# Expert layer of a hybrid decoder step: the last two experts' gate/up weights ahead of both their down weights

## The chip, the cores and the metric

The kernel runs on one core of a Trainium2 chip. The metric is the device time of one execution in microseconds; of the kernel before there are three runs. The profile is of one execution of its own, which is timed too.

## What is computed

The reference is one inference step of a decoder layer for 256 prompt tokens and 8 sample tokens of width 1024: a norm, an input projection, windowed attention beside a recurrent branch, an output projection, and then routed experts. Nearly all of the time goes to the experts. Each of the 264 tokens is sent to 4 of 32 experts; an expert is a clamped SwiGLU with float32 weights of 8 MiB (gate/up, 1024 x 2048) and 4 MiB (down, 1024 x 1024):

```python
h = xb @ w_gu[e] + b_gu[e]
g = jnp.minimum(h[:, 0::2], SWIGLU_LIMIT)
up = jnp.clip(h[:, 1::2], -SWIGLU_LIMIT, SWIGLU_LIMIT)
act = (up + 1.0) * (g * jax.nn.sigmoid(SWIGLU_ALPHA * g))
return act @ w_dn[e] + b_dn[e]
```

The results, times the gates, are added to the tokens' rows.

## The kernel before

Each expert is one item with room for 64 tokens (`CAP`); items 0 to 31 are the 32 experts in order, and a loop for experts with more tokens follows, whose count is read at run time. TensorE does for an item `q`, in this order (`item`, L1442):

- gate/up: 8 slots of weights, 64 records on two halves of the array's columns (L1451), and the bias (L1460);
- for the next item: the gather of its rows by one-hot matrices (`gather`, L1378 to L1389);
- the transposes of item `q`'s activations (L1472; the helper's line is L1114), then those of the next item's rows (`x_transposes`);
- in odd items: the placing of the results of items `q - 2` and `q - 1`, both at once, into the tokens' order (`place`, L1414 and L1422);
- down: 4 slots of weights, 32 records (L1492), into one PSUM bank.

Beside it VectorE computes the activation from gate/up's PSUM (L1060 to L1068, with ScalarE's sigmoid L617 between), copies the result of down out of PSUM (L1077, two copies of 64 rows; L1074, one copy of 128 rows, in the last item), makes the one-hot matrices of the next item, and adds placed results to the rows (L1045, L1047). ScalarE copies gathered rows (L608), transposed rows (L612, the operand of the next gate/up) and transposed activations (L621, the operand of down) out of PSUM. The last item, 31, is written out of the loop: it has no next item, and it places item 30's results between its gate/up and its transposes, while its activation is computed. Items 0 to 30 run in or around loops over pairs of items. After item 31 the result of the last item is copied and placed, added, and SP stores the rows.

The weights come through SP's queue, 1 MiB in each transfer. A ring has 8 slots for gate/up weights and 4 for the down weights of even items; the down weights of odd items have four places of their own (`extra`: parts of `regA`, `regC`, `regD`, `hT_t`). SP waits, slot by slot, on the count `m_used` of slots that TensorE has used (12 for each item): a gate/up slot of item `q` may be overwritten when gate/up of item `q - 1` has used it (`load_gu`, L316), a down slot when down of item `q - 2` has (`load_dn`, L322). SP runs its program in order. In the loop that is gate/up of an item and then down of the next one; the end is written out, gate/up 29, down 30, gate/up 30, gate/up 31, down 31.

Of the kernel before, what the change touches and what calls it, by code (L numbers as in the profile page):

```python
# [27 lines left out]
KT = D // P  # L28
# [11 lines left out]
E = 32  # L40
# [6 lines left out]
SLOTS = 12  # L47
# [9 lines left out]
N_PLACED = E // 2 + 2  # L57
# [16 lines left out]
def hybrid_layer(nc, a, o):  # L74

    ctx = ExitStack()
    with ctx:
# [33 lines left out]
        ps = ctx.enter_context(nc.psum_tensor("ps", [P, 8, 512], F32))  # L111
# [132 lines left out]
        def _(sp):  # L244
# [68 lines left out]
            def load_gu(q, e):  # L313

                for s in range(KT):
                    sp.wait_ge(m_used, q * SLOTS - (SLOTS - 1 - s))  # L316
                    load_slot(s, e)

            def load_dn(q, e, odd):

                for s in range(KT, SLOTS):
                    sp.wait_ge(m_used, q * SLOTS - (2 * SLOTS - 1 - s))  # L322
                    load_slot(s, e, odd)
# [5 lines left out]
                load_gu(p * 2 + 2, p * 2 + 2)  # L329
                load_dn(p * 2 + 3, p * 2 + 3, True)  # L330
            load_gu(E - 3, E - 3)
            load_dn(E - 2, E - 2, False)
            load_gu(E - 2, E - 2)
            load_gu(E - 1, E - 1)
            load_dn(E - 1, E - 1, True)
            sp.wait_ge(S["ovd"], 1)
            n_over = sp.value_load(ovi[0:1, 0:1], min_val=0, max_val=N_OVER)
# [326 lines left out]
        def _(dve):  # L664
# [313 lines left out]
            def choose_gates(q):  # L978
                dve.tensor_copy(tokg[:, :, 1:2], gate_cols[:, :, bass.ds(q, 1)]).then_inc(m_oh, 1)
# [59 lines left out]
            def add(n_placed, banks):  # L1039

                for i in (1, 2):
                    dve.wait_ge(m_pl, 3 * n_placed + i)
                    for n in range(2):
                        half = x_row[:, i, 512 * n:512 * n + 512]
                        dve.tensor_tensor(half, half, ps[:, banks[i - 1][n], :], ALU.add).then_inc(m_add, 1)  # L1045
                dve.wait_ge(m_pl, 3 * n_placed + 3)
                dve.tensor_tensor(x_s[:, :], x_s[:, :], ps[:, banks[2], 0:QW], ALU.add).then_inc(m_add, 1)  # L1047
# [3 lines left out]

            def item(q, ahead, r, n_placed):

                gu = ps[:, 1:3, :].rearrange("p n c -> p (n c)")
                if ahead:
                    dve.wait_ge(m_xg, q + 1)
                    choose_rows(q + 1)
                    choose_gates(q + 1)
                dve.wait_ge(m_gu, q + 1)
                dve.tensor_scalar(g_sb, gu[:, 0::2], LIMIT, None, ALU.min).then_inc(m_g, 1)  # L1060
                dve.tensor_scalar(up_sb, gu[:, 1::2], LIMIT, -LIMIT, ALU.min, ALU.max).then_inc(s_dve, 1)
                dve.wait_ge(m_g, q + 1)
                dve.wait_ge(s_dve, 2 * q + (base + 1))
                dve.scalar_tensor_tensor(out=up_sb, in0=up_sb, scalar=1.0, in1=g_sb,
                                         op0=ALU.add, op1=ALU.mult).then_inc(s_dve, 1)
                dve.wait_ge(s_dve, 2 * q + (base + 2))
                dve.wait_ge(m_sig, q + 1)
                dve.tensor_tensor(act_sb, up_sb, sig_sb, ALU.mult).then_inc(m_act, 1)  # L1068
                if n_placed is not None:
                    add(n_placed, beside_ahead if ahead else beside_last)  # L1070
                place_gates(q, r)
                dve.wait_ge(m_used, SLOTS * q + SLOTS)
                if r == whole:
                    dve.tensor_copy(y_sb[0][:, :], ps[:, 4, :]).then_inc(m_ysb, 2)  # L1074
                else:
                    for n in range(2):
                        dve.tensor_copy(y_sb[n][r, :], ps[64 * n:64 * n + 64, 4, :]).then_inc(m_ysb, 1)  # L1077
                dve.wait_ge(m_gated, q + 1)
                if ahead:
                    slots_of(q + 1, upper if r == lower else whole)  # L1080
                if n_placed is not None:

                    dve.wait_ge(m_add, n_placed * ADDS + ADDS)

            slots_of(0, upper)
            dve.wait_ge(s_tok, 32)
# [6 lines left out]
                item(p * 2 + 2, True, upper, None)  # L1093
            add(half, beside_ahead)
            dve.wait_ge(m_add, ADDS * half + ADDS)
            with dve.Fori(half, E // 2 - 1) as p:
                item(p * 2 + 1, True, lower, p + 1)
                item(p * 2 + 2, True, upper, None)
            item(E - 1, False, whole, N_PLACED - 2)
            n_over = dve.value_load(ovi[0:1, 0:1], min_val=0, max_val=N_OVER)  # L1100
            with dve.If(n_over > 0):
                with dve.Fori(0, n_over) as m:
# [9 lines left out]
        def _(pe):  # L1112
# [326 lines left out]
                                   bias_dn[:, QW * j:QW * j + QW], start=True, stop=True)  # L1439
                mm.then_inc(m_pl, 1)  # L1440

            def item(q, ahead, even, n_placed, alone, n_loads):  # L1442

                pe.wait_ge(m_xT, q + 1)
                for kt in range(KT):
                    pe.wait_ge(s_slot[kt], 16 * q + 16)
                    for n in range(2):
                        for h in range(2):  # L1450
                            mm = pe.matmul(ps[64 * h:64 * h + 64, 1 + n, :],  # L1451
                                           xT[:, kt % 4, 64 * (kt // 4):64 * (kt // 4) + 64],
                                           ring[:, kt, 1024 * h + 512 * n:1024 * h + 512 * n + 512],
                                           start=(kt == 0), stop=False)
                    mm.then_inc(m_used, 1)
                pe.wait_ge(s_bgu[0 if even else 1], n_loads * 32)
                for h in range(2):
                    for n in range(2):
                        r = slice(32 * n, 32 * n + 2)
                        mm = pe.matmul(ps[64 * h:64 * h + 64, 1 + n, :], sel[r, h, :],  # L1460
                                       b_gu[0 if even else 1][r, :],
                                       start=False, stop=True)
                mm.then_inc(m_gu, 1)
                if ahead:
                    pe.wait_ge(m_idx, q + 1)
                    gather(q + 1, whole if even else upper)
                else:

                    pe.wait_ge(m_idx, q + 1)
                    place(q - 1, beside_last, alone, lambda: pe.wait_ge(m_act, q + 1))  # L1470
                pe.wait_ge(m_act, q + 1)
                for j in range(4):  # L1472
                    mm = transpose(ps[:, 3, P * j:P * j + P], act_sb[:, P * j:P * j + P], P)
                mm.then_inc(m_atr, 1)

                def transposes_copied():
                    pe.wait_ge(m_aT, q + 1)
                    pe.wait_ge(m_xT, q + 2)

                if ahead:  # L1480
                    x_transposes(q + 1)
                    if n_placed is not None:
                        place(q - 1, beside_ahead, False, transposes_copied)

                pe.wait_ge(m_aT, q + 1)
                for s in range(4):
                    pe.wait_ge(s_slot[KT + s] if even else s_extra[s], n_loads * 16)
                    w = ring[:, KT + s, :] if even else extra[s]
                    for t in range(2):
                        h, j = divmod(2 * s + t, 4)  # L1490
                        for n in range(2):
                            mm = pe.matmul(ps[64 * n:64 * n + 64, 4, :], actT[:, j, 64 * h:64 * h + 64],  # L1492
                                           w[:, 1024 * t + 512 * n:1024 * t + 512 * n + 512],
                                           start=(s == 0 and t == 0), stop=(s == 3 and t == 1))
                    mm.then_inc(m_used, 1)
                if n_placed is not None:
                    pe.wait_ge(m_add, n_placed * ADDS + ADDS)

            pe.wait_ge(s_xns, 16 * 3)
            gather(0, upper)  # L1500
# [4 lines left out]
            mm.then_inc(S["gt_tr"], 1)  # L1505
            def pairs(p0, p1, biases):
                with pe.Fori(p0, p1) as p:
                    item(p * 2 + 1, True, False, p + biases if biases else p, False, p + 1)
                    item(p * 2 + 2, True, True, None, False, p + 2)

            pe.wait_ge(s_zero, 10)
            half = (E_BIAS - 1) // 2
            item(0, True, True, None, False, 1)
            pairs(0, half, 0)
            place_biases(beside_ahead)
            pe.wait_ge(m_add, ADDS * half + ADDS)
            pairs(half, E // 2 - 1, 1)
            item(E - 1, False, False, N_PLACED - 2, False, E // 2)
            pe.wait_ge(S["ovd"], 1)
            n_over = pe.value_load(ovi[0:1, 0:1], min_val=0, max_val=N_OVER)  # L1520
            with pe.If(n_over > 0):
                with pe.Fori(0, n_over) as m:
                    pe.wait_ge(m_idx, m + E)
                    gather(m + E, whole)
                    x_transposes(m + E)
                    item(m + E, False, True, m + (N_PLACED - 1), True, m + (E // 2 + 1))
            place(n_over + (E - 1), beside_last, True)


# [67 lines left out]
```

## Time and profile before

| | |
|---|---|
| median of 3 runs | 1151.42 us (1150.93 to 1152.32) |
| the profiled execution | 1153.59 us |
| its span, first to last instruction | 1151.7 us |
| granted TensorE clock, mean | 0.977 |
| TensorE (PE) busy | 1069.7 us, 93% of the span |
| its weight loads (PEld) | 439.4 us, 38% |
| VectorE (DVE), ScalarE (ACT), GpSimd (POOL) | 335.8, 140.0, 20.5 us |
| gate/up matmuls, L1451 | 2048 records, 461.2 us, 24.3 us idle before them |
| DMA | 422.10 MB, mean 367 GB/s |
| weight transfers from issue to landing | 20 to 22 us in the median |

The page says how busy an engine is on average; the stages have different limits, so what the change touches is read from the tail. A busy TensorE is not TensorE at its peak. In the rows, "PE L1451 x64" are 64 records of the matmul in line 1451 of the kernel, a bracket tells how long the engine was idle ahead of it and who ended that, and the chain follows back from the last instruction to what released each step. A granted clock of 1.00 is the upper of TensorE's two levels (2.4 GHz), 0.50 the lower (1.2 GHz).

### The profile page before, as it was taken

The page shows a single profiled execution, that of the slowest core. Times are in us where ns is not written, and L with a number is a line of the kernel's source. Part 1 is how long each engine was busy: PE and PEld are TensorE (multiplying, and loading weights), DVE is VectorE, ACT ScalarE, POOL GpSimd, SP SyncE. Part 2 cuts the span into 40 slices and gives each one's busy share as a digit, 9 for nine tenths or more (in the row PEclk, how much of TensorE's full clock was granted, in tenths as well). Part 3 has the DMA queues.
Part 4 walks back from the last instruction along what each step waited for, and adds up shares of the span by engine and source line. Part 5 has one row for each costly group of instructions (what it writes and reads, how often), then busy time and mean ns, then how long its engine had stood idle before and what let it go on. Part 6 is the DMA issues. An engine that isn't in the chain of part 4 may idle for free.

```text
span 1151.7 us, 14763 instructions
## 1 busy us (share of the span) xinstructions
PE 1069.7 (93%) x5498; PEld 439.4 (38%) x5498; DVE 335.8 (29%) x728; ACT 140.0 (12%) x264; POOL 20.5 (2%) x45
## 2 busy tenths in 40 slices
PE   3978888999999999999999899999998999999997
PEld 2866344333333333333333333333333333333332
DVE  2386448321212122222222212122121212121213
ACT  2227221000000000000000000000000000000000
POOL 5000000000000000000000000000000000000000
PEclk9998896999999998999999999999999999999999
DMA  8923217999999999999999999999999999999991
GB/s 254 377 100 69 99 48 291 405 417 418 418 420 418 420 418 420 418 418 418 419 417 419 417 419 417 420 417 420 416 420 417 419 419 418 420 418 420 415 415 53
DMA packets 83021, 422.10 MB, mean 367 GB/s; under 512 B 7458, under 2 KB 14906, under 8 KB 50215
## 3 DMA queue, kind: packets, MB, share of 16 engines
q1 hardware_dynamic: 81326, 418.25, 89.7%
q0 software_dynamic: 1232, 2.73, 0.8%
q10 hardware_dynamic: 440, 0.83, 0.2%
q8 instruction: 14, 0.23, 0.1%
q14 instruction: 9, 0.07, 0.0%
HBM read 420.46 MB, written 2.33 MB: 367 GB/s over the span
## 4 chain that ended last, share of the span: by engine, by line
PE 60%; DMA 22%; SPq 8%; DVE 4%; ACT 3%; issue 2%; DVEq 0%; ACTq 0%
PE ps L1451 22%; DMA ring<-in_w_gate_up_dram 20%; PE ps L1492 14%; SPq L273 8%; PE ps L1414 5%; PE ps L1378 4%; PE ps L1140 3%; PE ps L1273 3%; DMA regA<-in_w_in_dram 2%; PE ps L1460 2%; PE ps L1114 2%; PE ps L1389 1%; PE ps L1383 1%; ACT regA L608 1%; PE ps L1422 1%
## 5 line engine op out<-in xcount | busy, mean ns | idle before, releaser
L1451 PE MATMUL ps<-ring,regA 128*64 128x512 f32 x2048 | 461.2, 600 | 24.3 <-DMA ring<-in_w_gate_up_dram 22.4
L1451 PEld LDWEIGHTS ps<-ring,regA 128*64 128x64 f32 x2048 | 145.0, 138 | 334.5 <-issue 259.4
L1060 DVE TENSOR_SCALAR regA<-ps 128x512 f32<-128x512 f32 x32 | 22.1, 692 | 427.1 <-PE ps L1460 427.1
L617 ACT ACTIVATE regA<-regA 128x512 f32<-128x512 f32 x32 | 20.1, 630 | 798.9 <-DVE regA L1060 798.9
L1492 PE MATMUL ps<-ring,regA 128*64 128x512 f32 x512 | 113.4, 595 | 0.0
L1077 DVE COPY regA<-ps 64x512 f32<-64x512 f32 x62 | 42.7, 689 | 222.0 <-PE ps L1492 221.0
L1378 PE MATMUL ps<-regA 128*64 128x256 f32 x512 | 64.1, 393 | 0.0
L1045 DVE TENSOR_TENSOR x_row<-x_row,ps 128x512 f32<-128x512 f32 x72 | 46.1, 684 | 58.8 <-PE ps L1414 58.1
L1492 PEld LDWEIGHTS ps<-ring,regA 128*64 128x64 f32 x512 | 36.4, 137 | 65.8 <-issue 65.6
L1414 PE MATMUL ps<-regA 128*128 128x512 f32 (+1 forms) x136 | 59.7, 594 | 1.1 <-DVE regA L1074 1.1
L1140 PE MATMUL ps<-hT_t,regA 128*128 128x264 f32 x224 | 53.5, 399 | 3.7 <-DMA regA<-in_w_in_dram 3.7
L1114 PE MATMUL ps<-con,regA 128*128 128x128 f32 (+2 forms) x287 | 45.6, 283 | 6.7 <-ACT regA L608 6.7
L1378 PEld LDWEIGHTS ps<-regA 128*64 128x64 f32 x512 | 34.6, 139 | 39.8 <-issue 26.3
L1140 PEld LDWEIGHTS ps<-hT_t,regA 128*128 128x128 f32 x224 | 43.7, 198 | 11.8 <-issue 4.0
L1114 PEld LDWEIGHTS ps<-con,regA 128*128 128x128 f32 (+2 forms) x287 | 30.1, 141 | 15.5 <-issue 14.7
L1460 PE MATMUL ps<-regA,con 2*64 2x512 f32 x256 | 34.8, 613 | 0.0
L1414 PEld LDWEIGHTS ps<-regA 128*128 128x128 f32 (+1 forms) x136 | 23.8, 190 | 26.1 <-issue 26.1
L1492 PE MATMUL ps<-regA 128*64 128x512 f32 x128 | 31.0, 605 | 0.7 <-ACT regA L621 0.7
L1492 PE MATMUL ps<-regC,regA 128*64 128x512 f32 x128 | 30.2, 592 | 0.0
L1492 PE MATMUL ps<-hT_t,regA 128*64 128x512 f32 x128 | 30.2, 592 | 0.0
L1492 PE MATMUL ps<-regD,regA 128*64 128x512 f32 x128 | 30.2, 592 | 0.0
L608 ACT ACTIVATE regA<-ps 128x512 f32<-128x512 f32 x32 | 19.1, 597 | 64.6 <-PE ps L1389 64.6
(270 smaller groups left out, 635.8 us busy)
## 6 DMA issues: line engine op xcount, KB each, us to landing
ring<-in_w_gate_up_dram SPq DMA_DIRECT2D x256, 1024.0 KB, 20.7
ring<-in_w_down_dram SPq DMA_DIRECT2D x64, 1024.0 KB, 22.5
regA<-in_w_down_dram SPq DMA_DIRECT2D x16, 1024.0 KB, 19.4
regC<-in_w_down_dram SPq DMA_DIRECT2D x16, 1024.0 KB, 20.2
regD<-in_w_down_dram SPq DMA_DIRECT2D x16, 1024.0 KB, 21.0
hT_t<-in_w_down_dram SPq DMA_DIRECT2D x16, 1024.0 KB, 21.8
regA<-in_w_in_dram SPq DMA_DIRECT2D x7, 1024.0 KB, 12.1
regA<-in_w_out_dram SPq DMA_DIRECT2D x2, 1024.0 KB, 9.8
```

The lines of the kernel that those rows point to most:

```text
L273: sp.dma_start(ring[:, s, :], w_gu[bass.ds(e * D + s * P, P), :]).then_inc(s_slot[s], 16)
L608: act.activation(xg_sb.rearrange("p (h c) -> p h c", h=2), ps[:, 6:8, 0:QW], ACT.Copy).then_inc(m_xgs, 1)
L1045: dve.tensor_tensor(half, half, ps[:, banks[i - 1][n], :], ALU.add).then_inc(m_add, 1)
L1077: dve.tensor_copy(y_sb[n][r, :], ps[64 * n:64 * n + 64, 4, :]).then_inc(m_ysb, 1)
L1114: return pe.transpose(out, in_, ident[0:k, 0:k])
L1140: mm = pe.matmul(ps[:, PBANK[n], 0:T], w_in[:, kt, P * n:P * n + P], hT[:, kt, :], start=(kt == 0), stop=(kt == KT - 1))
L1273: mm = pe.matmul(ps[:, 2 * i - 2 + n, :], src[:, TOFF[i]:TOFF[i] + P], w_out[:, NC * half + c, 512 * n:512 * n + 512], start=(half == 0 an ...
L1378: pe.matmul(ps[64 * n:64 * n + 64, 6 + h, 0:QW], oneh[:, i, 0:CAP], xn_row[:, i, 512 * n + QW * h:512 * n + QW * h + QW], start=(i == 1), ...
L1414: mm = pe.matmul(ps[:, banks[i][n], :], gated[rows(n), P * i:P * i + P], y_sb[0 if alone else n][rows(n), :], start=True, stop=True)
L1451: mm = pe.matmul(ps[64 * h:64 * h + 64, 1 + n, :], xT[:, kt % 4, 64 * (kt // 4):64 * (kt // 4) + 64], ring[:, kt, 1024 * h + 512 * n:1024 ...
L1460: mm = pe.matmul(ps[64 * h:64 * h + 64, 1 + n, :], sel[r, h, :], b_gu[0 if even else 1][r, :], start=False, stop=True)
L1492: mm = pe.matmul(ps[64 * n:64 * n + 64, 4, :], actT[:, j, 64 * h:64 * h + 64], w[:, 1024 * t + 512 * n:1024 * t + 512 * n + 512], start=(s ...
```

## The change

SP's order of loading at the end becomes gate/up 29, gate/up 30, gate/up 31, down 30, down 31. TensorE, and VectorE with it, now end in a part of their own for the last two items (`last_two`): gate/up 30, gather of item 31, both transposes, gate/up 31, down 30, transposes of item 31's activations, placing of items 29 and 30, down 31. Item 29 is written out ahead of it, and the loop ends one pair earlier. The bodies of gate/up, of the transposes and of down become functions (`gate_up`, `act_transposes`, `down`; on VectorE `swiglu` and `y_copy`) that the loop and the new part share; in the loop and in the run-time loop the order stays what it was.

```diff
             load_gu(E - 3, E - 3)
-            load_dn(E - 2, E - 2, False)
             load_gu(E - 2, E - 2)
             load_gu(E - 1, E - 1)
+            load_dn(E - 2, E - 2, False)
             load_dn(E - 1, E - 1, True)
...
-            with dve.Fori(half, E // 2 - 1) as p:
+            with dve.Fori(half, E // 2 - 2) as p:
                 item(p * 2 + 1, True, lower, p + 1)
                 item(p * 2 + 2, True, upper, None)
-            item(E - 1, False, whole, N_PLACED - 2)
+            item(E - 3, True, lower, N_PLACED - 3)
+
+            def last_two():
+
+                dve.wait_ge(m_xg, E - 1)
+                choose_rows(E - 1)
+                choose_gates(E - 1)
+                swiglu(E - 2)
+                place_gates(E - 2, upper)
+                dve.wait_ge(m_gated, E - 1)
+                slots_of(E - 1, whole)
+                swiglu(E - 1)
+                dve.wait_ge(m_used, SLOTS * (E - 1) + KT)
+                y_copy(E - 2, upper)
+                add(N_PLACED - 2, beside_last)
+                place_gates(E - 1, whole)
+                dve.wait_ge(m_used, SLOTS * E)
+                y_copy(E - 1, whole)
+                dve.wait_ge(m_gated, E)
+                dve.wait_ge(m_add, (N_PLACED - 2) * ADDS + ADDS)
...
-            pairs(half, E // 2 - 1, 1)
-            item(E - 1, False, False, N_PLACED - 2, False, E // 2)
+            pairs(half, E // 2 - 2, 1)
+            item(E - 3, True, False, N_PLACED - 3, E // 2 - 1)
+
+            def last_two():
+
+                gate_up(E - 2, True, E // 2)
+                pe.wait_ge(m_idx, E - 1)
+                gather(E - 1, whole)
+                pe.wait_ge(m_act, E - 1)
+                act_transposes()
+                x_transposes(E - 1)
+                gate_up(E - 1, False, E // 2)
+                down(E - 2, True, E // 2)
+                pe.wait_ge(m_act, E)
+                act_transposes()
+                pe.wait_ge(m_idx, E)
+                place(E - 2, beside_last)
+                down(E - 1, False, E // 2)
+                pe.wait_ge(m_add, (N_PLACED - 2) * ADDS + ADDS)
```

## Rows read from the trace of the kernel before

**Rows 1.** Windows: stretch, us, busy (count) of PE, PEld, DVE, ACT, POOL; clock, DMA, GB/s.

```profile
340.00:1122.00 782.00, 752.83 (x3930) 274.53 (x3928) 178.99 (x378) 62.68 (x104) 0.00 (x0) 1.00 1.02 418
```

**Rows 2.** Chain of waits, 1040 us to the end: start us, us, what.

```profile
1044.60 25.91 DMA ring<-in_w_gate_up_dram
...
1088.92 13.82 PE ps L1451 x64
...
1108.48 7.04 PE ps L1492 x32
1115.51 13.73 PE ps L1451 x64
1129.25 1.02 PE ps L1460 x8
1130.26 3.63 PE ps L1414 x8
1133.89 0.57 PE ps L1422 x8
1134.46 0.60 PE ps L1114 x4
...
1135.09 0.61 ACT regA L621
...
1135.74 7.11 PE ps L1492 x32
```

**Rows 3.** Timeline of the tail: start us, us, instruction, [idle before it, releaser].

```profile
1100.80 0.20 PEld L1451 LDWEIGHTS ps<-ring,regA 128*64 128x64 f32 x4 [0.74 <-DMA ring<-in_w_gate_up_dram]
...
1108.52 0.60 ACT L612 ACTIVATE regA<-ps 128x512 f32<-128x512 f32 x1 [0.22 <-PE ps L1114]
...
1115.56 1.41 DVE L1077 COPY regA<-ps 64x512 f32<-64x512 f32 x2 [8.52 <-PE ps L1492]
...
1132.45 0.69 DVE L1068 TENSOR_TENSOR regA<-regA 128x512 f32<-128x512 f32 x1
...
1142.94 0.69 DVE L1074 COPY regA<-ps 128x512 f32<-128x512 f32 x1 [6.74 <-PE ps L1492]
...
1143.88 1.99 PE L1414 MATMUL ps<-regA 64*128 64x512 f32 x8 [1.05 <-DVE regA L1074]
```

**Rows 4.** Timeline of SP: issues of weights, first and last expert items.

```profile
197.76 12.69 SPq L273 DMA_DIRECT2D ring<-in_w_gate_up_dram  x8
...
1062.34 40.77 SPq L273 DMA_DIRECT2D ring<-in_w_gate_up_dram  x16
...
1090.68 0.33 SPq L273 DMA_DIRECT2D ring<-in_w_gate_up_dram  x1
...
1107.19 1.49 SPq L277 DMA_DIRECT2D hT_t<-in_w_down_dram  x1
```

**Rows 5.** DMA issues at 197.76, 210.12, 1075.38, 1090.68, 1107.19: last column, us to landing.

```profile
ring<-in_w_gate_up_dram SPq DMA_DIRECT2D x1, 1024.0 KB, 4.8
...
ring<-in_w_gate_up_dram SPq DMA_DIRECT2D x1, 1024.0 KB, 11.1
...
ring<-in_w_gate_up_dram SPq DMA_DIRECT2D x1, 1024.0 KB, 25.4
...
ring<-in_w_gate_up_dram SPq DMA_DIRECT2D x1, 1024.0 KB, 12.6
...
hT_t<-in_w_down_dram SPq DMA_DIRECT2D x1, 1024.0 KB, 23.3
```

**Rows 6.** Windows around the drop of the clock, and all behind it.

```profile
454.00:462.00 8.00, 6.96 (x20) 2.16 (x22) 1.45 (x6) 0.00 (x0) 0.00 (x0) 0.57 1.01 418
465.00:1147.00 682.00, 652.72 (x3410) 236.35 (x3406) 157.26 (x330) 54.27 (x90) 0.00 (x0) 1.00 0.98 404
```

**Rows 7.** Timeline of TensorE in 455 to 462.4.

```profile
455.04 7.87 PE L1451 MATMUL ps<-ring,regA 128*64 128x512 f32 x22 [1.44 <-DVE x_s L1047]
```

**Rows 8.** DMA queues in 1110 to 1145: packets, MB, share of 16 engines.

```profile
q8 instruction: 3, 0.05, 0.6%
```

More of the change, by code:

```diff
@@ L1052, in item @@
             def item(q, ahead, r, n_placed):
-                gu = ps[:, 1:3, :].rearrange("p n c -> p (n c)")
                 if ahead:
@@ L1058, in item, with swiglu @@
                     choose_gates(q + 1)
+                swiglu(q)
+                if n_placed is not None:
+                    add(n_placed, beside_ahead if ahead else beside_last)
+                place_gates(q, r)
+                dve.wait_ge(m_used, SLOTS * q + SLOTS)
+                y_copy(q, r)
+                dve.wait_ge(m_gated, q + 1)
+                if ahead:
+                    slots_of(q + 1, upper if r == lower else whole)
+                if n_placed is not None:
+                    dve.wait_ge(m_add, n_placed * ADDS + ADDS)
+            def swiglu(q):
+                gu = ps[:, 1:3, :].rearrange("p n c -> p (n c)")
                 dve.wait_ge(m_gu, q + 1)
@@ L1068, in item, with y_copy @@
                 dve.tensor_tensor(act_sb, up_sb, sig_sb, ALU.mult).then_inc(m_act, 1)
[L1069 to L1072, printed above, removed]
+            def y_copy(q, r):
                 if r == whole:
@@ L1077, in item @@
                         dve.tensor_copy(y_sb[n][r, :], ps[64 * n:64 * n + 64, 4, :]).then_inc(m_ysb, 1)
[L1078 to L1083, printed above, removed]
             slots_of(0, upper)
@@ L1095, in _ @@
             dve.wait_ge(m_add, ADDS * half + ADDS)
-            with dve.Fori(half, E // 2 - 1) as p:
+            with dve.Fori(half, E // 2 - 2) as p:
                 item(p * 2 + 1, True, lower, p + 1)
                 item(p * 2 + 2, True, upper, None)
-            item(E - 1, False, whole, N_PLACED - 2)
+            item(E - 3, True, lower, N_PLACED - 3)
[16 more added lines that the diff above has]
+                dve.wait_ge(m_add, (N_PLACED - 2) * ADDS + ADDS)
+            last_two()
             n_over = dve.value_load(ovi[0:1, 0:1], min_val=0, max_val=N_OVER)
@@ L1440, in place_biases, with item, transposes_copied, gate_up @@
                 mm.then_inc(m_pl, 1)
-            def item(q, ahead, even, n_placed, alone, n_loads):
+            def item(q, ahead, even, n_placed, n_loads):
+                gate_up(q, even, n_loads)
+                if ahead:
+                    pe.wait_ge(m_idx, q + 1)
+                    gather(q + 1, whole if even else upper)
+                pe.wait_ge(m_act, q + 1)
+                act_transposes()
+                def transposes_copied():
+                    pe.wait_ge(m_aT, q + 1)
+                    pe.wait_ge(m_xT, q + 2)
+                if ahead:
+                    x_transposes(q + 1)
+                    if n_placed is not None:
+                        place(q - 1, beside_ahead, False, transposes_copied)
+                down(q, even, n_loads)
+                if n_placed is not None:
+                    pe.wait_ge(m_add, n_placed * ADDS + ADDS)
+            def gate_up(q, even, n_loads):
                 pe.wait_ge(m_xT, q + 1)
@@ L1463, in item, with act_transposes @@
                 mm.then_inc(m_gu, 1)
[L1464 to L1471, printed above, removed]
+            def act_transposes():
                 for j in range(4):
@@ L1474, in item, with down @@
                 mm.then_inc(m_atr, 1)
[L1476 to L1483, printed above, removed]
+            def down(q, even, n_loads):
                 pe.wait_ge(m_aT, q + 1)
@@ L1495, in item @@
                     mm.then_inc(m_used, 1)
-                if n_placed is not None:
-                    pe.wait_ge(m_add, n_placed * ADDS + ADDS)
             pe.wait_ge(s_xns, 16 * 3)
@@ L1507, in pairs @@
                 with pe.Fori(p0, p1) as p:
-                    item(p * 2 + 1, True, False, p + biases if biases else p, False, p + 1)
-                    item(p * 2 + 2, True, True, None, False, p + 2)
+                    item(p * 2 + 1, True, False, p + biases if biases else p, p + 1)
+                    item(p * 2 + 2, True, True, None, p + 2)
             pe.wait_ge(s_zero, 10)
             half = (E_BIAS - 1) // 2
-            item(0, True, True, None, False, 1)
+            item(0, True, True, None, 1)
             pairs(0, half, 0)
@@ L1516, in _ @@
             pe.wait_ge(m_add, ADDS * half + ADDS)
-            pairs(half, E // 2 - 1, 1)
-            item(E - 1, False, False, N_PLACED - 2, False, E // 2)
+            pairs(half, E // 2 - 2, 1)
[10 more added lines that the diff above has]
+                pe.wait_ge(m_act, E)
+                act_transposes()
+                pe.wait_ge(m_idx, E)
+                place(E - 2, beside_last)
+                down(E - 1, False, E // 2)
+                pe.wait_ge(m_add, (N_PLACED - 2) * ADDS + ADDS)
+            last_two()
             pe.wait_ge(S["ovd"], 1)
@@ L1525, in _ @@
                     x_transposes(m + E)
-                    item(m + E, False, True, m + (N_PLACED - 1), True, m + (E // 2 + 1))
+                    gate_up(m + E, True, m + (E // 2 + 1))
+                    pe.wait_ge(m_idx, m + (E + 1))
+                    place(m + (E - 1), beside_last, True, lambda: pe.wait_ge(m_act, m + (E + 1)))
+                    pe.wait_ge(m_act, m + (E + 1))
+                    act_transposes()
+                    down(m + E, True, m + (E // 2 + 1))
+                    pe.wait_ge(m_add, (m + (N_PLACED - 1)) * ADDS + ADDS)
             place(n_over + (E - 1), beside_last, True)
```

## The prediction

> **What bounds the kernel now.** I read the windows first, then the chain of waits, then the timeline of its last 110 us, and last the issues of the weight queue. From 340 to 1122 us the DMA share is 1.02 at 418 GB/s [rows 1]: in the expert loop the transfers set the pace, and one weight transfer of 1 MiB is worth 2.51 us (1.0486 MB at 418 GB/s). The place that matters is the tail, where this stops. The chain runs through a weight transfer for the last time until 1044.60 + 25.91 = 1070.5 us, the last gate/up slot of item 29 [rows 2]. From 1088.92 to 1135.06 it is TensorE's work, broken only by short copies of ScalarE: gate/up 30 in 13.82 us, down 30 in 7.04, gate/up 31 in 13.73, placing of item 30 in 3.63 + 0.57, four transposes in 0.60 [rows 2]. Then TensorE waits for ScalarE's copy of the transposed activations (1135.06 to 1135.74, 0.68 us), and down 31 runs to 1135.74 + 7.11 = 1142.85 [rows 2]. The one wait on a transfer in all this is that of a weight load at 1100.80 [rows 3]; the last transfer is issued at 1107.19 and takes 23.3 us [rows 4, 5], so it lands at 1130.5, five us before down 31 begins. So the tail is bound by TensorE and by the copies between its steps, and the change has to be priced there.
>
> **The change, part by part.** The profiled execution took 1153.59 us with a span of 1151.7, 1.9 us lying around it; it is 2.2 above the median of the runs shown, 1151.42. I work out a difference and add it to both.
>
> *Everything up to 1088.92 stays.* Items 0 to 28 keep their loop, and item 29 does the same work written out. The four transfers of down 30 leave their place behind gate/up 29 in SP's queue, so they can't delay that item, whose last slot lands at 1070.5 as before. Gate/up 30 is now issued straight behind it, and each of its slots waits until gate/up 29 has used the slot; item 29 uses a slot in 1.7 us (8 of 64 records at 13.73 us [rows 2]) after it lands, so when its first slot comes free the queue still holds transfers for most of the time up to 1070.5. I cost this at nothing: its cover is the queue itself. If the cover fails, it costs TensorE nothing before the 18 us between 1070.5 and 1088.92 are used up.
>
> *Gate/up 30 comes four transfers earlier.* Now its last slot is issued at about 1075.38 and lands 25.4 us later, at 1100.8 [rows 5], just when it is wanted; this makes the piece 13.82 us where the same 64 records of item 31 take 13.73 [rows 2]. Four transfers earlier is 1090.7, ten us before it is wanted. Gain 0.09. (No more: the rest of that wait is a weight load that runs ahead of its matmul.)
>
> *The weight queue runs dry.* Gate/up 31 may be issued only when gate/up 30 has used its first slot, at 1090.68 [rows 4], with the new order as with the old. Before, four transfers were still under way at that time and the first slot took 12.6 us to land [rows 5]; now the queue has just emptied, and SP has nothing else that it could issue, since the eight gate/up slots stand ahead of both down weights in its program. How a restart goes is shown at 197.76: eight gate/up transfers into an empty queue, issued behind the matmuls over 12.69 us, the first landing after 4.8 us and the last, issued at 210.12, after 11.1 [rows 4, 5], so 23.5 us from first issue to last landing. Put at 1090.68 this lands gate/up 31 by 1114.1, down 30 from 1116.7 to 1124.2 and down 31 from 1126.7 to 1134.2, at 2.51 us each. The end of the transfers thus moves from 1130.5 to 1134.2. It is hidden as long as TensorE wants them later, which the next steps show. The far bounds: no restart cost at all, which nobody would see either, and gate/up 31 landing no earlier than before, which is a rival below.
>
> *Gate/up 31 moves ahead of down 30.* Before, the transposes of item 31's rows end at 1108.48, TensorE goes on with down 30, and ScalarE's copy of them (1108.52, 0.60 us) lies beside it [rows 2, 3]. Now gate/up 31 comes next and must wait for that copy. The nearest row is the wait for a copy of the same form at 1135: 0.68, and 0.07 for the refill (7.11 against 7.04) [rows 2]. Bounds: 0.60, the copy alone, and 1.3, if ScalarE still had another of its passes in hand; its copy of item 30's activations is over by then, so I take 0.75. Behind it in TensorE's order stands all that is left, gate/up 31, down 30 and what VectorE waits for from them. With the 0.09 gained it starts at 1109.07 and ends at 1122.87; with the 1.0 us of the bias, down 30 runs from 1123.9 to 1130.9. Gate/up 31 wants its last slot at 1121 (landed 1114), down 30 its first at 1123.9 (1116.7) and its fourth 5.3 us on, at 1129.2 (1124.2): the smallest margin is 5.0 us.
>
> *The activation of item 31 is covered.* VectorE's four steps and the sigmoid end at 1132.45 + 0.69, 3.9 us behind gate/up's bias at 1129.25 [rows 2, 3]; now they have the 7.04 us of down 30 beside them. The transposes of item 31 follow down 30 at once, and ScalarE's copy of them lies beside the placing of item 30. So the wait of 0.68 and its refill of 0.07 go: gain 0.75.
>
> *The result of item 30 is late next.* Down 30 used to be followed by 13.73 us of gate/up 31, under which VectorE's two copies out of PSUM lay (1115.56, 1.41 us) [rows 3]. Now the placing of item 30 stands four short transposes behind down 30 and needs both copies; queued behind it in TensorE's order are the placing itself and all of down 31. From the end of a down piece to the end of the copies is 1.46 us (1115.51 to 1116.97), and from a copy's end to the placing 0.25 us (1143.63 to 1143.88, the same pair at the very end) [rows 2, 3]; less 0.60 of transposes, TensorE waits 1.11, and 0.07 for the refill. Bounds: 0.5, if one of the two copies were enough, and 1.8, if the transposes hid none of it. I take 1.18. VectorE itself is idle by then. The additions and item 31's gate placing, which VectorE now does behind these copies, have the 7 us of down 31 beside them. ScalarE's program stays, GpSimd has no part in the tail, and SP's stores wait for the additions behind down 31, as before.
>
> **Sum**: −0.09 + 0.75 − 0.75 + 1.18 = +1.09 us. Down 31 starts at 1132.64 + 0.07 + 3.63 + 0.57 = 1136.9 (its weights landed by 1134.2) and ends at 1143.95 in place of 1142.85; all behind that is as before. Span 1152.8, the profiled execution 1154.7, the median 1151.42 + 1.09 = **1152.5 us**. Against 0.2% (2.3 us), about what a measurement of this kernel can tell from no change, this is no change, on the slow side.
>
> **Rivals.**
> *The clock falls in the new waits (slower).* After the placing of the biases and a wait of 1.44 us the granted clock is 0.57 over 454 to 462, and 22 gate/up records take 7.87 us [rows 6, 7] where 22 of the 64 that take 13.73 are worth 4.72: 3.15 lost. From 465 to 1147 it is 1.00 throughout [rows 6], through the short matmuls and transposes before each item and through the waits of 0.68 at 1135 and 1.05 at 1143 [rows 2, 3]. The new place is the stretch before gate/up 31: the same short work as in every item, now 0.7 us longer. If that takes the clock to its lower level, gate/up 31 runs as the 22 records did: 1.09 + 3.15, 1155.7. The Trainium skill (TensorE: Matmul & The Clock Gate, Why this matters for your kernels) says that idle gaps between bursts of matmuls throttle TensorE again; the drop at 454 agrees with it, and the gaps at 1135 and 1143, which left the clock at 1.00, show that not every gap does. 10%.
> *The restart is slower than the one at 197.76 (slower).* If gate/up 31 landed no earlier than before, its last slot came at 1120.7, and down 30's fourth at 1130.7, 1.5 us after it is wanted: +2.6, 1154.0. It decides from 5 us of delay on. Against it stands that the queue holds nothing else. 6%.
> *Code has to be fetched.* Items 29 and 30, so far in the loop, are written out. Three instruction loads in 1110 to 1145 take 0.6% of 16 engines' 35 us [rows 8], 1.1 us each; two exposed ones make +3.3, 1154.7. Against it: gate/up 31, already the first written-out piece, follows down 30 without a gap [rows 2]. 3%.
> *Both new waits are covered.* Then only the gains are left: −0.84, 1150.6. It needs an order of TensorE other than the one written, for nothing but 0.60 us stands between down 30 and the placing. 6%.
>
> **How the numbers follow.** 75% for the forecast, with the chances above for the rest. The bounds of the two waits put the forecast alone at 1151.6 to 1153.7. The covered case and the slow restart widen this to 1150.6 and 1154.0, and the runs of the kernel before, which lie within −0.5 and +0.9 of their median, to 1150.5 and 1154.2; the clock's and the code's cases stay outside (13%). Slower by over 0.2% (1153.7) are the clock, most of the restart's and the code's cases: 17%. Faster by over 0.2% (1149.1) is reached by none of them; I leave it 2% for what I don't see. Within: 81%.
>
> **What would show it.** Right: a wait of about 0.7 us of TensorE on ScalarE's copy before gate/up 31; one of about 1.1 on VectorE's copies before the placing of item 30; none before down 31; a dip of the DMA share shortly after 1090; the last weights landing near 1134; down 31 ending 1.1 us later. Wrong: a weight transfer in the chain after 1070, a granted clock under 1.00 between 1100 and 1143, holes of TensorE that no wait explains between 1055 and 1109, or a placing of item 30 that starts right behind the transposes.

## The result, and the profile after

The changed kernel takes 1154.88 us in the median of 20 runs (1152.67 to 1158.07), the kernel before 1152.83 in the median of 20 (1150.18 to 1154.67). The ratio is 1.0018, with a 95% interval of 1.0011 to 1.0026: 2.05 us slower, 1.3 to 3.0. The forecast was +1.09 us and 1152.5. Of the miss of 2.4 us, 1.4 is the base: the three runs that I added to had a median of 1151.42, the longer series 1152.83. The other 1.0 is the change itself, and this is what the experiments are about. The profiled execution took 1154.22 us with a span of 1152.3. Spans of single executions differ by more than the change moves: in the 20 runs of the changed kernel they lie between 1150.8 and 1156.1. So I compare the stretch that the change touches, from the start of gate/up 30 to the end of down 31. Before, it is 1088.92 to 1142.85, 53.93 us [rows 2].

The chain of waits of the changed kernel, from the last gate/up transfer of item 29 on (start us, us, what; L1501 is gate/up, L1529 down, L1143 the transposes, L1443 the placing, which takes the results of items 29 and 30 in one go):

```profile
1042.57 25.81 DMA ring<-in_w_gate_up_dram
...
1086.80 13.73 PE ps L1501 x64
...
1106.31 0.60 ACT regA L612
...
1106.96 15.65 PE ps L1501 x64
...
1123.63 7.02 PE ps L1529 x32
1130.64 0.59 PE ps L1143 x4
1131.23 0.97 issue
1132.20 3.67 PE ps L1443 x8
...
1136.44 7.04 PE ps L1529 x32
```

The order is gate/up 30, gate/up 31, down 30, transposes, placing, down 31, and the last transfer in the chain is still that of item 29. The stretch is 1086.80 to 1143.48, 56.68 us, 2.75 longer than before [rows 2]. That it starts 2.1 us earlier than in the profile of before is none of the change's doing as far as I can see: the work up to there is the same, and the first gate/up weights of the loop are issued at 196.12 us here and at 197.76 before [rows 4], so that 1.6 us of it are there while the first expert still runs.

The same tail in the timeline (start us, us, instruction, and in brackets the idle time ahead of it with its releaser):

```profile
1106.96 15.65 PE L1501 MATMUL ps<-ring,regA 128*64 128x512 f32 x64 [0.69 <-ACT regA L612]
...
1130.69 1.41 DVE L1091 COPY regA<-ps 64x512 f32<-64x512 f32 x2 [4.18 <-PE ps L1529]
...
1132.20 3.67 PE L1443 MATMUL ps<-regA 128*128 128x512 f32 x8 [0.97 <-issue]
```

Both new waits are where the forecast put them: 0.69 us for ScalarE's copy before gate/up 31, and 0.97 before the placing. The profile puts the second one down to nothing ("issue"), but it ends 0.10 us after VectorE's two copies (1130.69 + 1.41). What was not in the sum is in the piece between them: the 64 records of gate/up 31 took 15.65 us in place of 13.73 [rows 2]. The windows of this stretch say why (length, busy time and count of PE, PEld, DVE, ACT and POOL, granted clock, DMA share, GB/s):

```profile
1086.80:1107.20 20.40, 19.52 (x113) 7.63 (x110) 5.55 (x13) 2.41 (x4) 0.00 (x0) 1.00 0.86 336
1107.20:1110.60 3.40, 3.40 (x10) 0.97 (x8) 0.00 (x0) 0.00 (x0) 0.00 (x0) 0.50 1.01 413
1110.60:1143.50 32.90, 31.89 (x148) 10.38 (x144) 7.30 (x12) 1.23 (x2) 0.00 (x0) 1.00 0.65 261
```

For 3.4 us from 1107.2 on, which begins 0.24 us after gate/up 31 started, the granted clock was 0.50, the lower of the two levels, and 10 records were issued in it; at the upper level one is worth 0.21 us [rows 2]. The rival of the falling clock is what happened in this execution.

The weight queue: SP's last issue in its timeline, then the landing times of the transfers issued at 1088.56 (the first of gate/up 31) and 1114.03 (the last of all; last column, us to landing), then the window behind 1088:

```profile
1114.03 2.97 SPq L277 DMA_DIRECT2D hT_t<-in_w_down_dram  x1
```

```profile
ring<-in_w_gate_up_dram SPq DMA_DIRECT2D x1, 1024.0 KB, 4.8
```

```profile
hT_t<-in_w_down_dram SPq DMA_DIRECT2D x1, 1024.0 KB, 18.8
```

```profile
1088.00:1100.00 12.00, 12.00 (x60) 3.94 (x56) 1.17 (x6) 0.00 (x0) 0.00 (x0) 1.00 0.85 313
```

It went as forecast. Gate/up 31's first slot lands 4.8 us after its issue into the empty queue, the DMA share of 1088 to 1100 falls to 0.85, and the last transfer lands at 1114.03 + 18.8 = 1132.8, before down 31 starts at 1136.4; the forecast was 1134.2.

### The profile page after: what moved, and what is told of

It is laid out like the page before. It is cut to its first block, busy times and chain, and to the rows that moved or that the text cites. A ratio compares the mean times of both kernels' runs of the same rounds, so it can differ in the third digit from the quotient of the medians.

```text
span 1152.3 us, 14729 instructions
## 1 busy us (share of the span) xinstructions
PE 1068.2 (93%) x5498; PEld 439.4 (38%) x5498; DVE 335.9 (29%) x728; ACT 139.8 (12%) x264; POOL 20.4 (2%) x45
## 4 chain that ended last, share of the span: by engine, by line
PE 59%; DMA 22%; SPq 9%; DVE 4%; ACT 3%; issue 2%; DVEq 0%; ACTq 0%
PE ps L1501 22%; DMA ring<-in_w_gate_up_dram 20%; PE ps L1529 14%; SPq L273 8%; PE ps L1443 5%; PE ps L1407 4%; PE ps L1169 3%; PE ps L1302 3%; DMA regA<-in_w_in_dram 2%; PE ps L1510 2%; PE ps L1143 2%; PE ps L1418 1%; ACT regA L608 1%; PE ps L1412 1%; PE ps L1451 1%
## 5 line engine op out<-in xcount | busy, mean ns | idle before, releaser
L1501 PE MATMUL ps<-ring,regA 128*64 128x512 f32 x2048 | 462.4, 602 | 25.1 <-DMA ring<-in_w_gate_up_dram 22.3
L1501 PEld LDWEIGHTS ps<-ring,regA 128*64 128x64 f32 x2048 | 145.9, 138 | 334.9 <-issue 259.4
L1529 PE MATMUL ps<-ring,regA 128*64 128x512 f32 x512 | 113.4, 596 | 0.0
L1529 PEld LDWEIGHTS ps<-ring,regA 128*64 128x64 f32 x512 | 36.4, 137 | 66.4 <-issue 66.3
L1443 PE MATMUL ps<-regA 128*128 128x512 f32 (+1 forms) x136 | 59.6, 595 | 2.0 <-DVE regA L1088 1.1
L1143 PE MATMUL ps<-con,regA 128*128 128x128 f32 (+2 forms) x287 | 45.0, 280 | 6.7 <-ACT regA L608 6.7
L1143 PEld LDWEIGHTS ps<-con,regA 128*128 128x128 f32 (+2 forms) x287 | 29.8, 139 | 15.7 <-issue 15.0
L1443 PEld LDWEIGHTS ps<-regA 128*128 128x128 f32 (+1 forms) x136 | 23.9, 190 | 26.4 <-issue 26.4
L1529 PE MATMUL ps<-regA 128*64 128x512 f32 x128 | 31.0, 605 | 0.0
L1529 PE MATMUL ps<-hT_t,regA 128*64 128x512 f32 x128 | 30.2, 592 | 0.0
L1529 PE MATMUL ps<-regD,regA 128*64 128x512 f32 x128 | 30.2, 592 | 0.0
L1529 PE MATMUL ps<-regC,regA 128*64 128x512 f32 x128 | 30.2, 592 | 0.0
L1143 PE MATMUL ps<-con,ring 128*128 128x128 f32 (+4 forms) x64 | 11.9, 313 | 16.4 <-DVE ring L687 16.4
```

Of the source, the lines that this page charges most:

```text
L1143: return pe.transpose(out, in_, ident[0:k, 0:k])
L1443: mm = pe.matmul(ps[:, banks[i][n], :], gated[rows(n), P * i:P * i + P], y_sb[0 if alone else n][rows(n), :], start=True, stop=True)
L1501: mm = pe.matmul(ps[64 * h:64 * h + 64, 1 + n, :], xT[:, kt % 4, 64 * (kt // 4):64 * (kt // 4) + 64], ring[:, kt, 1024 * h + 512 * n:1024 ...
```

## The experiments

Theory 1: the change costs two new waits, net about 1 us, and some 1.9 us more (15.65 against 13.73) in those executions in which the clock falls before gate/up 31. Its rivals were that the queue which runs dry costs the time, and that the two waits are all and the drop is rare chance. In each verdict the numbers in us are the ratio's interval times 1152.7.

**The old order of loading under the new order of computing (old_queue).**

```diff
             load_gu(E - 3, E - 3)
+            load_dn(E - 2, E - 2, False)
             load_gu(E - 2, E - 2)
             load_gu(E - 1, E - 1)
-            load_dn(E - 2, E - 2, False)
             load_dn(E - 1, E - 1, True)
```

> The changed kernel with SP's order of loading as before (down 30 ahead of gate/up 30 again); TensorE and VectorE keep the new order. Theory 1 (the change costs the two new waits, some 1.0 us net, and 1.9 us more in the executions in which the clock falls before gate/up 31): nothing changes against the changed kernel, +1 to +3 us against the kernel before, no wait of TensorE on a transfer behind 1071. Rival (the queue that runs dry costs the time): the dip of the DMA share after 1088 goes and the time falls to at most +1 us against the kernel before.

Measured: ratio 1.0029, 1.0017 to 1.0041 (+2.0 to +4.7 us). The DMA share in a window, what TensorE's matmuls waited for between 1080 and 1146 (us in total, times, longest), and the chain at gate/up 30 (its first 56 records), gate/up 31 and down 31:

```profile
1088.00:1100.00 12.00, 12.00 (x58) 4.02 (x56) 2.29 (x7) 0.00 (x0) 0.00 (x0) 1.00 1.01 414
```

```profile
PE ps L1443 <- issue: 1.0, 1, 1.0
PE ps L1501 <- ACT regA L612: 0.7, 1, 0.7
```

```profile
1089.05 12.02 PE ps L1501 x56
...
1109.44 15.65 PE ps L1501 x64
...
1138.93 7.04 PE ps L1529 x32
```

The dip of the DMA share is gone, no matmul waits for a transfer, and by its time the kernel is not faster than the changed one. Gate/up 31 took 15.65 us in this profile too, and the stretch is 1089.05 to 1145.97, 56.92 us, 0.24 longer than in the changed kernel: a weight load of gate/up 30 waits 0.90 us for its transfer, as one does in the kernel before [rows 3], and that piece takes 13.97 us. So the queue that runs dry is not what costs the time; the new order of loading is worth about a quarter of a microsecond in the profiles, too little for the times to tell, and the order of computing is what costs.

**The bias of gate/up 31 first (bias_first).**

```diff
...
+                bias(0, 0, True)
+                bias(0, 1, True)
+                bias(1, 0, True)
+                pe.wait_ge(m_xT, q + 1)
+                for kt in range(KT):
...
+                bias(1, 1, False).then_inc(m_gu, 1)
...
```

`bias(n, h, first)` is one of the four bias matmuls; the last one stands behind the weights as before.

> The changed kernel, with three of gate/up 31's four bias matmuls issued ahead of its weights, while TensorE waits for ScalarE's copy of the transposed rows. Theory 1: the wait of 0.69 us before gate/up 31 goes and 0.7 us with it; if the idle time is what brings the clock down, the clock stays at 1.00 too and the kernel stands at +0.3 us against before; if the lack of dense matmuls is (the bias has two rows), the drop can still come and it stands at up to +2. Rival (waits alone, the drop seen in one profile is rare): +0.3 us, no drop.

Measured: ratio 1.0024, 1.0013 to 1.0035 (+1.5 to +4.0 us). The chain behind the transposes (L1519 is the bias, L1532 gate/up 31), and a window:

```profile
1107.19 1.01 PE ps L1519 x6
1108.20 15.58 PE ps L1532 x64
1123.79 1.00 PE ps L1519 x2
```

```profile
1108.30:1111.70 3.40, 3.40 (x10) 0.99 (x10) 0.00 (x0) 0.00 (x0) 0.00 (x0) 0.50 1.00 410
```

The wait is gone, but the 0.7 us did not come: torn apart, the bias takes 1.01 + 1.00 us where it took 1.02 in one piece [rows 2], which I had not foreseen. And the clock fell all the same: it was 0.50 for 3.4 us from 1108.3 on, and gate/up 31 took 15.58 us, right behind 1.01 us of bias matmuls of two rows. So an idle wait ahead of the dense piece is not needed for the drop; the one wait left in the short work, 0.19 us ahead of the last four transposes, stands there in the kernel before too. The Trainium skill (TensorE: Matmul & The Clock Gate, Why this matters for your kernels) warns of idle gaps between bursts of matmuls; no such gap stands ahead of gate/up 31 here.

**A discarded dense matmul in the wait (dense_fill).**

```diff
                 x_transposes(E - 1)
+                pe.matmul(ps[:, 4, :], con[:, 0:P], xn_row[:, 1, 0:512], start=True, stop=True)
                 gate_up(E - 1, False, E // 2)
```

> The changed kernel with one more matmul of 128x128 by 128x512, whose result is thrown away, between the transposes of item 31's rows and gate/up 31; it adds work of about 0.86 us where the wait is 0.69. Theory 1: no drop of the clock before gate/up 31, so the mean comes down although work is added: +1.2 us against before, gate/up 31 in 13.8 us. Rival (waits alone): 0.2 us slower than the changed kernel, and so above +2.

Measured: ratio 1.0003, 0.9993 to 1.0013 (-0.8 to +1.5 us). Its chain (L1563 is the added matmul), and the window of the stretch:

```profile
1085.54 13.73 PE ps L1501 x64
...
1105.01 0.86 PE ps L1563 x2
1105.87 13.88 PE ps L1501 x64
...
1128.38 0.97 issue
...
1133.59 7.04 PE ps L1529 x32
```

```profile
1085.50:1140.70 55.20, 53.95 (x270) 18.86 (x266) 12.85 (x25) 3.64 (x6) 0.00 (x0) 1.00 0.77 305
```

With 0.86 us of useless work in place of 0.69 us of waiting, gate/up 31 is back at 13.88 us, the clock is 1.00 all through the stretch, and this is 1085.54 to 1140.64, 55.10 us. The kernel is not to be told from the one before by its time, and its interval meets that of the changed kernel only between 1.0011 and 1.0013; from that of old_queue, which has the same order of computing and was measured against the same runs of the kernel before, it is apart (1.0013 and 1.0017). The rival of the waits alone had it slower than the changed kernel.

**The same wait in every even item of the kernel before (pair_wait).**

```diff
                         place(q - 1, beside_ahead, False, transposes_copied)
+                    else:
+                        pe.wait_ge(m_xT, q + 2)
```

> The kernel before, with one wait more in every even item: down waits until ScalarE has copied the transposed rows of the next item, 15 copies of the changed kernel's wait in one execution. Items up to 28 are paced by transfers, so only item 30's wait shows in the time. Theory 1: the granted clock falls to 0.50 behind some of the 15 waits, down pieces there take longer, and the time is +0.7 us, or +2 to +3 where item 30 is hit. Rival (the drop is rare): no drop in 15 waits, +0.7 us.

Measured: ratio 1.0023, 1.0012 to 1.0034 (+1.4 to +3.9 us). There are 16 such waits, since item 0 has one as well. First what TensorE waited for (total, times, longest), then windows at two of the five at which the clock fell, and one long window between two of the five:

```profile
PE ps L1494 <- ACT regA L612: 12.2, 16, 0.8
```

```profile
571.60:575.00 3.40, 3.10 (x8) 1.03 (x10) 0.00 (x0) 0.17 (x1) 0.00 (x0) 0.50 1.01 420
...
1110.90:1114.30 3.40, 2.87 (x8) 1.03 (x10) 0.00 (x0) 0.40 (x1) 0.00 (x0) 0.50 1.02 424
575.00:868.00 293.00, 282.87 (x1494) 104.41 (x1490) 68.02 (x145) 23.51 (x39) 0.00 (x0) 1.00 1.02 418
```

Behind 5 of the 16 waits of at most 0.8 us the clock was at 0.50 for some 3.4 us, the last time in item 30. In the kernel before, the same short work without a wait stands ahead of the down pieces of all 16 even items; in its profile the clock is 1.00 over 465 to 1147 [rows 6] and ahead of the placing of the biases as well:

```profile
200.00:450.00 250.00, 248.27 (x1328) 94.26 (x1325) 64.73 (x145) 21.70 (x36) 0.00 (x0) 1.00 1.02 417
```

The time is higher than I can account for: item 30's wait of 0.8 us and a drop in 5 of 16 cases make about 1.3 us, and the interval begins at 1.4. Where the rest comes from stays open.

**The same with a dense matmul in each wait (pair_dense).** The line added to pair_wait is that of dense_fill, ahead of the wait.

> The kernel before with the wait for the transposed rows in all 15 even items as in pair_wait, where the clock fell behind 5 of them, but now with a discarded matmul of 128x128 by 128x512 in the wait. Theory 1: the clock falls behind none of the 15, and the time is +0.9 us (item 30's 0.86 us of work) where pair_wait stood at +2.9. Rival (the wait itself costs, whatever TensorE does in it; the drops were chance): still some drops, +2 to +3 us.

Measured: ratio 1.0018, 1.0006 to 1.0030 (+0.7 to +3.5 us). The windows on both sides of the placing of the biases, at which the clock falls in every kernel:

```profile
200.00:453.00 253.00, 251.28 (x1327) 94.44 (x1323) 65.47 (x146) 21.69 (x36) 0.00 (x0) 1.00 1.01 415
465.00:1149.00 684.00, 659.47 (x3434) 239.32 (x3430) 158.13 (x331) 54.24 (x90) 0.00 (x0) 1.00 0.98 404
```

No drop behind any of the 16. The time does not confirm it as well as the profile does: the interval holds the expected +0.9, but also the +2.7 of pair_wait, so by time the two aren't told apart. The mean granted clock over all executions does tell them apart, and shows that the profiles are no chance picks: it is 0.973 over the 12 executions of pair_wait, 0.979 over the 12 of pair_dense, and 0.979 over the 35 of the kernel before beside either. A drop of 3.4 us at 0.50 lowers the mean of one execution by 0.0015 (1.7 us of 1155), so the waits bring about four drops in an execution, and none that shows when they hold a dense matmul.

**The changed kernel again (after_again).**

> The changed kernel once more, beside the others of this call. Theory 1 (two new waits, net 1 us, and 1.9 us more in the executions in which the clock falls before gate/up 31): +1.3 to +3 us against before; in the profile either gate/up 31 in 15.6 us behind a clock of 0.50, or in 13.8 with the clock at 1.00. Rival (two waits alone): +1 us.

Measured: ratio 1.0019, 1.0007 to 1.0031 (+0.8 to +3.6 us). The chain of its profile:

```profile
1089.02 13.73 PE ps L1501 x64
...
1109.18 13.95 PE ps L1501 x64
...
1131.76 0.97 issue
...
1136.97 7.04 PE ps L1529 x32
```

No drop this time: gate/up 31 in 13.95 us, and the stretch is 1089.02 to 1144.01, 54.99 us, 1.06 longer than before. This is the forecast sum of 1.09 in an execution in which the clock stayed; that it is met to 0.03 us is in part luck, as the list further down shows.

**How often it falls (count_1, count_2, count_3).** Three more profiles of the changed kernel, one execution each.

> The changed kernel, one more profile, to see how often the clock falls before gate/up 31. Theory 1: either 56.7 to 56.9 us from gate/up 30 to the end of down 31 with a clock of 0.50 in it, or 55.0 without; a mean of +2 us would want the first in about half of the executions. Rival (rare drop, something else costs): 55.0 without a drop in nearly all.

> As count_1: 56.7 to 56.9 us with a drop or 55.0 without; theory 1 about half each, rival nearly always 55.0.

> As count_1: 56.7 to 56.9 us with a drop or 55.0 without; theory 1 about half each, rival nearly always 55.0.

Measured: 1154.11, 1154.63 and 1152.76 us in single runs. One window of each, in this order:

```profile
1107.40:1110.80 3.40, 3.40 (x10) 0.97 (x8) 0.00 (x0) 0.00 (x0) 0.00 (x0) 0.50 0.99 407
```

```profile
1089.00:1144.00 55.00, 53.11 (x266) 18.58 (x262) 12.85 (x25) 3.64 (x6) 0.00 (x0) 1.00 0.76 307
```

```profile
1105.40:1108.80 3.40, 3.13 (x8) 1.01 (x10) 0.00 (x0) 0.22 (x1) 0.00 (x0) 0.50 1.01 422
```

Drop, no drop, drop. With the first profile and after_again that makes 3 of 5. By the chains the stretch took 56.68, 56.69 and 56.53 us with the drop, and 54.99 in both profiles without: a drop costs 1.5 to 1.7 us. 1.06 + 3/5 of 1.65 is 2.05 us, which is what the 20 runs show; that it meets so well is luck, since five profiles are few, and the interval of 1.3 to 3.0 allows for any share from a seventh up. The mean granted clock of the 12 executions of after_again, 0.978 against 0.979 in the 35 of the kernel before beside them, fits a share like this and is too coarse to fix it.

**A longer wait (pair_wait_long).** pair_wait, with one more pass of ScalarE, into unused columns, ahead of its copy of the transposed rows.

> pair_wait with one more copy of ScalarE ahead of that of the transposed rows, so that the wait in the even items is 1.3 us in place of 0.69. If the length of the stretch without dense matmuls decides, more of the 15 waits are followed by a drop of the clock than the 5 of pair_wait. Rival (drops come by chance, of no matter what length): about 5 again.

Measured: 1152.93 us in one run. The waits, and the windows of its drops:

```profile
PE ps L1495 <- ACT regA L613: 19.9, 16, 1.2
```

```profile
512.70:516.10 3.40, 2.94 (x8) 1.03 (x10) 0.00 (x0) 0.33 (x1) 0.00 (x0) 0.50 1.02 425
864.30:871.10 6.80, 5.98 (x14) 1.76 (x16) 0.00 (x0) 0.69 (x2) 0.00 (x0) 0.50 1.01 418
925.70:929.10 3.40, 3.04 (x8) 1.03 (x10) 0.00 (x0) 0.23 (x1) 0.00 (x0) 0.50 1.02 425
```

Three drops behind 16 waits of 1.2 us, one of them twice as long, against five behind waits of 0.8. My expectation that a longer wait brings more drops is not borne out; with one profile of each, three and five are not told apart either, and what picks the waits that are hit stays open.

**One copy in place of two before the placing (dense_half).** dense_fill, and the following (ScalarE's part for the last item is written out for it; only its two new lines are marked):

```diff
             act.wait_ge(m_g, E)
             act.activation(sig_sb, g_sb, ACT.Sigmoid, scale=ALPHA).then_inc(m_sig, 1)
+            act.wait_ge(m_used, SLOTS * (E - 1) + KT)
+            act.activation(y_sb[1][64:128, :], ps[64:128, 4, :], ACT.Copy).then_inc(m_ysb, 1)
...
-                y_copy(E - 2, upper)
+                dve.tensor_copy(y_sb[0][upper, :], ps[0:64, 4, :]).then_inc(m_ysb, 1)
```

> dense_fill, and ScalarE copies one half of item 30's result while VectorE copies the other, so that the placing of items 29 and 30 waits for one copy in place of two. Theory 1: the wait before the placing falls from 0.97 to 0.3 us, the stretch from gate/up 30 to the end of down 31 is 0.7 us shorter than in dense_fill (55.1), 54.4, and the kernel is +0.5 us against before. Rival (the placing waits for something else, such as code): 0.97 stays.

Measured: ratio 0.9993, 0.9982 to 1.0004 (-2.1 to +0.5 us). Its chain:

```profile
1088.56 13.73 PE ps L1507 x64
...
1131.39 0.25 issue
...
1135.88 7.04 PE ps L1535 x32
```

The wait ahead of the placing falls from 0.97 to 0.25 us, and the stretch to 1088.56 to 1142.92, 54.36. So it was VectorE's second copy that the placing waited for.

**Half of down 30 in the wait (split_down).** The old order of loading, the halved copy of dense_half, and:

```diff
                 x_transposes(E - 1)
+                down(E - 2, True, E // 2, (0, 1))
                 gate_up(E - 1, False, E // 2)
-                down(E - 2, True, E // 2)
+                down(E - 2, True, E // 2, (2, 3))
```

> The changed kernel with before's order of loading, the first two slots of down 30 multiplied ahead of gate/up 31 and the last two behind it, and ScalarE copying half of item 30's result. The wait for the transposed rows is filled with work that has to be done anyhow. Theory 1: no wait before gate/up 31, no drop of the clock, 53.5 us from gate/up 30 to the end of down 31 where the kernel before takes 53.9; -0.4 us against before, which is no change. Rival (the drop comes of the short work before it, with or without the wait): gate/up or down there at 0.50 and +1.5 us.

Measured: ratio 1.0004, 0.9993 to 1.0016 (-0.8 to +1.8 us). Its chain (L1507 gate/up, L1535 down):

```profile
1088.03 13.83 PE ps L1507 x64
...
1107.60 3.58 PE ps L1535 x16
1111.18 13.73 PE ps L1507 x64
...
1134.59 7.04 PE ps L1535 x32
```

No wait before gate/up 31, 13.73 us for it, and 1088.03 to 1141.63, 53.60 us for the stretch: 0.33 less than before, the forecast 0.4. That is too little for its time to show, and neither this version nor dense_half beats the kernel before. Once the last slot of item 29 has landed, the tail is TensorE's work, and no order of it that I tried takes more than a third of a microsecond away.

## Why the prediction was wrong

The sum of the steps stands, and the step that failed is a term that was left out of it: the rival "If that takes the clock to its lower level", which got 10% and no share of the 1.09 us. The clock did fall in 3 of 5 profiles. The reason that I gave against it, the short work before each item and two waits elsewhere at which the clock held, looked at each by itself; the new stretch joined such work and such a wait, and in pair_wait that was enough for 5 of 16. The price was off the other way: I took 3.15 us from 8 us at a mean clock of 0.57 [rows 6], that is 6.9 us at 0.50; the drops here last about 3.4 and cost 1.5 to 1.7. Together they are worth 1.0 us in the mean, just what the measured difference has over the forecast one.

A second term was mis-sized, the base: the median of three runs and their spread, 1150.93 to 1152.32, stood for a kernel whose 20 runs have a median of 1152.83 and reach from 1150.18 to 1154.67. With the clock's case left out and a base 1.4 us too low, the range ended 0.7 us short of the median measured. On the longer base the same range would have ended at 1155.6 and held it, clock and all; that would have been luck, since the mechanism was missing from the sum either way. (The lower bound of the two waits adds up to 1151.7 and not to 1151.6, which moves nothing.)

Point by point, in the profile without the drop (after_again):

- *Everything up to gate/up 30 stays*: right; the last transfer in the chain is still item 29's.
- *Gate/up 30 comes earlier, 0.09*: right, 13.73 us.
- *The queue runs dry at no cost*: right; old_queue, without the dip, is no faster.
- *Gate/up 31 waits for the copy, 0.75*: 0.67 of wait, and the refill made the piece 13.95 in place of 13.73, so 0.89: the refill is 0.22 and not the 0.07 taken from down 31.
- *The activation is covered, -0.75*: right; down 31 takes 7.04 us without a wait.
- *The result of item 30 is late, 1.18*: 0.97, and 0.04 of refill, so 1.01. The hand-over from VectorE's copy took 0.11 us and not 0.25. This miss and that of the copy, −0.17 and +0.14, cancel in the sum.
- *Code* and *slow restart*: not seen. No hole without a wait, and in the first profile of the changed kernel the first landing after 4.8 us as at 197.76 [rows 5].

That the drop is caused by what TensorE does in that stretch is shown by dense_fill (it goes when the wait holds a dense matmul, and the time with it) and by pair_dense beside pair_wait (no drop in place of five, and the mean clock of all executions with it); that the share is 3 in 5 is only counted, not explained.

## What to carry to other kernels

When a step is moved, look at what TensorE does in the few microseconds ahead of it: short matmuls, transposes and a wait for a copy may each be harmless and together bring the clock down, and the price stands in the next dense piece, not in the wait. Where a wait of this kind can't be avoided, fill it with dense matmuls, best with some that have to be done anyhow, as split_down does. And in a tail that no transfer holds up, a new order of the transfers has next to nothing to give (0.09 to 0.24 us here), and a copy that the new order of computing brings out from under a long matmul piece is paid for (0.89 and 1.01 us here).

## What the runs showed of the hardware

The clock fell to 0.50 in bias_first with no idle time ahead of the dense piece, behind two-row matmuls; it stayed at 1.00 through the same stretch in dense_fill. The same program had the drop in some executions and not in others, so that one profile alone would have told either story: 56.68 or 54.99 us for one and the same stretch. Four bias matmuls on four parts of PSUM took 1.02 us together, but three and one apart took 1.01 and 1.00.
